# The first token tile alone up to its experts, the second beside the first expert slots, in a two-part transformer kernel

## Time and profile before

| what | value |
|---|---|
| median of 3 runs | 1614.35 us |
| profiled execution, whole | 1615.83 us |
| its span, first to last instruction | 1614.0 us |
| granted clock of TensorE, mean | 0.964 of full |
| busy: PE, DVE, ACT, POOL | 84%, 69%, 33%, 24% |
| moved by DMA | 433.17 MB, 268.45 MB of it by the gathers |

### The profile page before, as it was taken

One profiled execution on the slowest core, in us unless ns is written; L12 is line 12 of the kernel. 1 busy time (PEld: TensorE's weight loads), 2 busy tenths in 40 slices (PEclk: granted clock), 3 DMA queues, 4 the chain that ended last, 5 costly groups with the idle time before them and its releaser, 6 DMA issues.

```text
span 1614.0 us, 17165 instructions
## 1 busy us (share of the span) xinstructions
PE 1358.5 (84%) x6258; PEld 952.2 (59%) x6258; DVE 1108.2 (69%) x2039; ACT 532.0 (33%) x1030; POOL 384.5 (24%) x329
## 2 busy tenths in 40 slices
PE   5999788888876776777777779978999989899997
PEld 5887566444432222222232248857999878689996
DVE  6575588888656776888865565557756578767654
ACT  1443344332212112212221133543543254435430
POOL 1000003444433444444444401100111034001110
PEclk8899899999999999999999999989999999999999
DMA  9554528999999998999999954325545534255540
GB/s 365 211 209 157 209 79 323 381 411 399 421 413 382 418 422 340 422 420 422 421 411 422 422 222 157 105 79 185 209 168 198 185 131 139 97 196 196 195 170 26
DMA packets 116628, 433.17 MB, mean 268 GB/s; under 512 B 6832, under 2 KB 7088, under 8 KB 83520
## 3 DMA queue, kind: packets, MB, share of 16 engines
q0 software_dynamic: 36864, 268.45, 40.4%
q1 hardware_dynamic: 79392, 162.51, 28.3%
q10 hardware_dynamic: 288, 1.11, 0.2%
HBM read 431.00 MB, written 1.05 MB: 268 GB/s over the span
## 4 chain that ended last, share of the span: by engine, by line
PE 47%; DMA 25%; DVE 20%; ACT 5%; issue 2%; POOL 1%; SPq 0%; DVEq 0%; ACTq 0%; POOLq 0%
PE PS L1360 33%; DMA EB<-in_experts,EI 23%; DVE EB L2375 5%; DVE WL L2056 4%; PE PS L1560 4%; PE PS L1561 3%; PE PS L1345 2%; PE PS L1356 1%; PE PS L1343 1%; DVE LNV L2079 1%; DMA W<-in_w_ada 1%; DVE XL L2064 1%; ACT BIG L1878 1%; ACT WH L1702 1%; PE PS L1403 1%
## 5 line engine op out<-in xcount | busy, mean ns | idle before, releaser
L2652 POOL DMA_INDIRECT EB<-in_experts,EI x256 | 293.8, 1148 | 574.7 <-PE PS L1561 332.0
L1560 PE MATMUL PS<-EB,BIG 128*128 128x512 f32 x512 | 284.1, 637 | 161.1 <-ACT BIG L1878 160.8
L2375 DVE CUSTOM_DVE_ANT_0 EB<-EB,Y 128x1024 f32<-128x1024 f32 x256 | 313.5, 1225 | 139.1 <-DMA EB<-in_experts,EI 138.5
L2056 DVE TENSOR_TENSOR WL<-W,WH 128x1024 fp32r<-128x1024 f32 x232 | 299.3, 1338 | 100.7 <-ACT WH L1702 100.3
L1560 PEld LDWEIGHTS PS<-EB,BIG 128*128 128x128 f32 x512 | 89.5, 196 | 321.9 <-ACT BIG L1878 269.3
L1561 PE MATMUL PS<-EB,BIG 128*128 128x512 f32 x512 | 270.4, 611 | 0.0
L1702 ACT ACTIVATE WH<-W 128x1024 fp32r<-128x1024 f32 x232 | 229.5, 1048 | 80.1 <-PE PS L1356 73.3
L1360 PE MATMUL PS<-XH,WH 128*128 128x256 f32 x768 | 221.5, 288 | 6.1 <-DVE WL L2056 5.4
L1360 PE MATMUL PS<-XL,WH 128*128 128x256 f32 x768 | 216.7, 282 | 0.0
L1360 PE MATMUL PS<-XH,WL 128*128 128x256 f32 x792 | 215.2, 286 | 0.0
L1561 PEld LDWEIGHTS PS<-EB,BIG 128*128 128x128 f32 x512 | 100.4, 196 | 128.7 <-issue 128.7
(11 more groups left out here) (328 smaller groups left out, 1725.3 us busy)
## 6 DMA issues: line engine op xcount, KB each, us to landing
W<-in_ffn_w SPq DMA_DIRECT2D x32, 2048.0 KB, 8.7
W<-in_w_ada SPq DMA_DIRECT2D x12, 2048.0 KB, 13.1
W<-in_w_in SPq DMA_DIRECT2D x6, 2048.0 KB, 14.1
W<-in_hy_w_in SPq DMA_DIRECT2D x6, 2048.0 KB, 10.9
W<-in_gla_w_in SPq DMA_DIRECT2D x6, 2048.0 KB, 8.0
W<-in_w_query SPq DMA_DIRECT2D x4, 2048.0 KB, 10.5
W<-in_w_out SPq DMA_DIRECT2D x2, 2048.0 KB, 8.0
EB<-in_experts,EI POOLq DMA_INDIRECT x256, 10.9
```

The costliest lines, as they stand in the source:

```text
L1560: e.matmul(PS[u[0][0]][:, :], DG[i], rows_up[:, 1024:1536], start=start, stop=stop)
L2056: e.tensor_tensor(tile.lo[:, k, :], tile.w[:, k, :], tile.hi[:, k, :].bitcast(F32), ALU.subtract).then_inc(*VE.up(("lo", tile.index, n)))
L2375: e.tensor_tensor_reduce(out=u, in0=u, in1=Y[:, s // 128, :], scale=1.0, scalar=0.0, op0=ALU.mult, op1=ALU.add, accum_out=dots[:, s:s + 1] ...
L2652: e.indirect_dma_start(out=EBUF[i], out_offset=None, in_=A["experts"][:, :], in_offset=bass.IndirectOffsetOnAxis(ap=EI[:, t, j:j + 1], axi ...
```

## The change

- The fox heads are done per token tile: `forgetting(t, u)` does only the causal block of tile 0 (128 columns) or the 256 columns of tile 1. Tile 0's run stays in the hooks of win[5]. The tile's own norm, output products, x1 and transposes follow at once, and then its first two query tiles. Tile 1's sb half of the output product stands before tile 0's x1 is turned.
- Tile 1's fox heads, norm, output, x1 and all other query products and scores become one list of steps, `second_way`, of which the slot loop takes one at every even slot below 20, one at each of slots 20 to 42 and 50 to 56, and one at every even slot from 58 on; the list ends at slot 100.
- The output and query weights are no longer split: `wout_part` and `query_product` multiply float32 as it is, from one copy XT of the turned activations. A query product has the weights stationary, so its result is already turned, and the copy and four turns behind the first product go.
- Query tiles 1 and 2 are loaded as halves into the upper parts of two buffers by `load_query`; query tiles 0 and 3 share one buffer.
- The gathers use a ring of six buffers in slots 0 to 25; the two others, where the fox heads' data lies, join at slot 26 (JOIN).
- The late modulation tiles (`late_rows`) stand behind tile 1's first choice instead of ahead of it.
- Small moves: the keys are loaded earlier, the final gain at slot 112 instead of 76, clearing of query buffers is four writes instead of two.

```diff
+JOIN = 26
...
+        in_buf, had_buf, ring, last_slot = [], [], collections.deque(range(6)), {}
+        for s in range(SLOTS):
+            if s == JOIN:
+                ring.extendleft((7, 6))
+            b = ring.popleft()
+            ring.append(b)
...
-            norm_x1 = Norm("x1", do.x1_piece, x1_stats, do.x1_apply, Y)
-            later_split(wq[0])
...
+            square, first, second = fox_norm_steps(0, fox_u, lambda: at(4))
+            square()
             for j in range(2):
+                wout_group(j, 0, bank())
+            first()
+            second()
+            for j in range(2):
+                wout_rest(j, 0)
+                do.x1_piece(j, groups[j, 0], 0, ("tm", wout[j].index, 0))
+            for j in range(2):
+                wout_group(j, 1, at(6 + j))
+            x1_stats(0)
+            do.x1_apply(0)
+            x1_turned(0)
+            do.load_query(1)
...
+            def second_tile():
+                u = bank()
+                o.filling.add(u[0])
+                yield from forgetting(1, u)
+                square, first, second = fox_norm_steps(1, u, bank)
+                square()
+                o.filling.discard(u[0])
+                yield
+                first()
+                yield
+                second()
+                yield
+                for j in range(2):
+                    wout_rest(j, 1)
+                    yield
+                    do.x1_piece(j, groups[j, 1], 1, ("tm", wout[j].index, 1))
+                    yield
+                do.load_query(2)
+                x1_stats(1)
+                yield
+                do.x1_apply(1)
+                yield
+                x1_turned(1)
+                yield
+
+            def second_way():
+                yield from second_tile()
+                for t, j in ((0, 2), (1, 0), (0, 3), (1, 1), (1, 2), (1, 3)):
+                    yield from query(t, j, blocks=1)
...
-                for step in beside.pop(s, ()):
-                    step()
-                if s == 76:
+                if s < 20 and s % 2 == 0 or 20 <= s < 43 or 50 <= s < 57 or s > 57 and s % 2 == 0:
+                    next(way, None)
+                if s == 112:
                     do.fetch_gf()
...
-                    if t == 0:
-                        for j in (10, 11):
-                            yield from late_rows(j)
+                        if (t, h) == (1, 0):
+                            for j in (10, 11):
+                                yield from late_rows(j)
...
+            def wout_part(j, t, u, half):
...
+                for k in range(4 * half, 4 * half + 4):
+                    x, w = XT[:, k, block(t)], tile.w[:, k, :]
...
+                        e.matmul(PS[u[0]][:, :], x, w, start=k == 0, stop=False)
...
+            def query_product(t, j, i, u):
...
+                mm(PS[u[0]][:, block(i)], [(query_rows(j, k)[:, block(i)], XT[:, k, block(t)]) for k in range(8)], *names)
...
+            def fox_scores(h, t, u):
+                j = 2 * h + t
+                dve.wait_ge(TE, ("fox scores", t, h))
+                e.tensor_reduce(MXA[:, j:j + 1], PS[u[0]][:, 0:128 * (t + 1)], X_AXIS, ALU.max, negate=True).then_inc(
+                    *VE.up(("fox max", t, h)))
```

More of the change, by code:

```diff
@@ L695, in program, with put_v @@
             steps = collections.deque(head_norm_steps("sb", 1, values["sb"], gain=gain_sb, to=0)[:7])
+            passes = [0]
             def fox_pass():
-                if next(fox, True):
-                    return False
+                for _ in range((2, 1, 3, 2)[passes[0]]):
+                    next(fox, None)
+                passes[0] += 1
                 if len(steps) > 2:
                     steps.popleft()()
[L702 to L706, removed]
+            def put_v(u, t):
+                do.put_tokens(VF[t], win[5], t, u)
+                do.note(("v fox", t))
+            tm_tile(win[5], put_v, hook=fox_pass, n=3)
+            while steps:
+                steps.popleft()()
+            for _ in fox:
+                pass
+            while o.behind:
+                tick()
             groups = {}
@@ L710, in wout_group, with wout_rest, fox_norm_steps, square @@
                 groups[j, t] = u
[L711 to L721, removed]
-            assert not steps and len(groups) == 2
-            fox_steps = head_norm_steps("fox", 0, values["fox"], gain=gain_fox, to=1)
-            do.note("att")
-            tick(3)
-            for step in fox_steps[:4]:
-                step()
-            do.fetch_keys()
+                o.filling.add(u[0])
+                do.wout_part(j, t, u, 0)
+            def wout_rest(j, t):
+                u = groups[j, t]
+                do.wout_part(j, t, u, 1)
+                o.filling.discard(u[0])
+                if t:
+                    close_tile(wout[j])
+            def fox_norm_steps(t, u, to_bank):
+                k = slice(8 * t, 8 * t + 8)
+                hs, hr, ht = (a[:, 0:16] for a in (hs_, hr_, ht_))
+                def square():
+                    do.heads_write("fox", t, u)
+                    do.heads_square("fox", 0, t, u)
+                def first():
+                    do.heads_sums("fox", 0, t, u, 8, hs)
+                    do.rsqrt_first(("fox", t), hr[:, k], hs[:, k], 8 / 512, 1e-6, None)
+                def second():
+                    do.rsqrt_second(("fox", t), hr[:, k], hs[:, k], ht[:, k])
+                    do.heads_scale("fox", 0, t, 8, hr)
+                    turn_whole(to_bank(), Y[:, t, :], t, 0, ("ready", "fox", t), ("xt", "fox", t), gain_fox, 1)
+                return [square, first, second]
             def x1_stats(t):
@@ L892, in program @@
+            def second_way():
+                yield from second_tile()
+                for t, j in ((0, 2), (1, 0), (0, 3), (1, 1), (1, 2), (1, 3)):
+                    yield from query(t, j, blocks=1)
+            way = second_way()
+            next(way)
+            choice = choices()
             for _ in range(21):
                 next(choice)()
-            beside = collections.defaultdict(list)
-            for n, step in zip((1, 2, 3, 3, 4), (copy[1], keys[0], put[0], keys[1], put[1])):
-                beside[n].append(step)
@@ L962, in program @@
                     split_piece(hyt[0])
-            assert nu == SLOTS and chosen and not beside
+            assert nu == SLOTS and chosen and next(way, None) is None
             o.held = None
```

484 lines of the change are left out of this document (230 added, 254 removed).

## The result

The changed kernel takes 1633.28 us (median of 4 runs, 1629.37 to 1636.13), the one before 1614.34 beside it. The ratio is 1.0116, with a 95% interval of 1.0094 to 1.0137: slower, where -7 us was forecast. The profiled execution took 1633.01 us with a span of 1631.2, so the span grew by 17.2 us.

What follows compares the result with a forecast made beforehand. The prediction took the expert stage as bound by the gathers, 2.49 us a slot. Its terms, -28 + 9.5 + 11.5 + 7 - 7 = -7, gave 1606.5 us; the 8-in-10 range was 1589 to 1625.

Steps and rivals of the forecast that it cites:

- Term 1: Stage ahead of the slots: first gather at 224 us instead of 252.15, -28 us (bounds 218 and 232).
- Term 2: Slots 0 to 20, one tile 1 fox step per slot pair: rounds of 8 us, +9.5 us (bounds -6 and +20).
- two ups are 3.42 us: In each round of slots 0 to 20, PE's two up products take 3.42 us, ending at 6.8 us.
- the first dot comes 7 us after the first gather: At slot 0: 7 us, not 10.5, since no query tile is being loaded then.
- E + 3.4: In a round, E is the end of a head's scores on PE; ACT's diagonal, needed by the odd slot's up, ends 3.4 us later.
- rival B: Slots 0 to 57: hand-overs between DVE, PE and ACT take more than the front won; slower, 1628 us, 22% chance.
- Term 3: Slots 20 to 29, tile 1's norm, output and x1 read serially: 34 us against 22.3, +11.5 us (bounds 0 and +20).
- waits about 6 us: DVE in slots 20 to 29: waits for the turn 1, two output products 1.5 each, squares and root 2 us.
- the root with its table: In slots 20 to 29, DVE's wait for squares and the root including its table load: 2 us.
- term 4: Slots 29 to 57, query steps one a slot make PE exceed the gathers: +7 us together (bounds 0 and +13).
- term 5: Slot 128: POOL's wait for tile 1's first choice goes, -7 us with the refill behind it.
- The rule on the drain: Table switches on ACT: a 1.38 us drain beside the 1.28 load, 1.4 us more a round, 1616 us; 3 in 100.

Runs made afterwards that it cites:

- e2: The changed kernel with each tile 1 head's values product repeated six more times on PE while it waits for the diagonal; 1628.97 us, ratio 1.0079.
- e4: The changed kernel with tile 1's fox maxima, exponentials and copies one step behind their scores, in eleven steps instead of ten; 1618.31 us, ratio 1.0014.
- e5: The changed kernel with all ten fox steps of tile 1 between the choice steps ahead of slot 0; 1620.12 us, ratio 1.0032 to the kernel before.
- e7: e5 with tile 1's norm, output and x1 steps at every third slot from 1, and the last two buffers joining at slot 10; 1608.11 us, ratio 0.9958.
- e10: e7 with the seventh and eighth buffer joining at slot 26, as in the changed kernel, instead of 10; 1614.42 us, ratio 0.9994.
- e6: The changed kernel with copies in place of logarithm and exponential in tile 1's fox norm and x1 roots (wrong values); 1632.39 us, ratio 1.0107.
- e12: The changed kernel with only the query steps moved, one at every odd slot from slot 29 on; 1641.80 us, ratio 1.0166 to the kernel before.
- e1: The kernel before with one edit: late modulation rows stand behind tile 1's first choice of experts; 1609.30 us, ratio 0.9968.
- e3: The changed kernel with Square in place of Gelu in the slots, so no table change in the rounds; 1615.55 us, ratio 1.0001.

## Why the prediction was wrong

**Term 1 was right**, in its sub-steps too: x1's sum at 200.20 (200), the first maximum at 211.97 (212), the gather at 223.74 (224). The earlier sub-steps were within 2 us: PE ends the product that closes tile 9 at 182.5 (180.5) and the two sb halves at 189.4 (189).

**Term 2 failed, mis-sized by 16.6 us, in the steps "two ups are 3.42 us" and "the first dot comes 7 us after the first gather".** The first one: the prediction followed the round at full clock, though the same text has PE held until E + 3.4 for a diagonal, and its own rows showed a product twice as long behind idle time. It had used that for term 1 and for rival B only. The five regular pairs take 45.9 us from dot 4 to dot 14, not 40: 5.9 us, of which 4.9 go when PE is kept busy (e2).

The second one is 4.5 us: dot 0 is at +11.5. I had put the wait before down to a load of a query tile, but DVE works on the 21 steps of choice right up to its first dot, before and after, and no row of the trace has it wait for a transfer there. In the changed kernel one fox step stands ahead of these choices, and DVE, in its order, takes the maximum of head 0 first. Its scores stand on PE behind the second query tile:

```profile
226.51 0.42 DVE L2255 TENSOR_REDUCE ST<-PS 128x1 f32<-128x256 f32 x1 [3.70 <-PE PS L1549]
```

This wait of 3.70 us, and one of 0.73 behind it for the gates' exponential on ACT, are as long as the miss. No run takes them away: in e4 this maximum stands later, but DVE then waits 3.23 us for the exponential, and dot 0 comes 1.6 us sooner.

The other 6.2 us are 4.0 in slots 14 to 20, at 3.2 us and not 2.5, and 2.2 that are left for the first two pairs. No run parts the causes of slots 14 to 20: they take 17.0 to 19.6 us in e2 to e5 as well. DVE waits there twice for rows (1.58 and 1.16 us) and once for a gelu (1.98), and e7, with two more buffers, takes 17.6 us where e10 takes 21.0. The forecast's own sum is loose here, too: from +54, six slots at 2.5 end at +69, not +72.5. By its own steps term 2 would have been +6.

**Term 3 failed, the step "waits about 6 us"**: the waits were 11.8 us, and the term was mis-sized by 6.1. DVE's own work was right: 39.9 us less its waits of 11.8 leave 28.1, and 27.4 had been counted. The waits on DVE in this stretch (time, times, longest):

```profile
DVE XT L2120 <- PE PS L1432: 4.3, 1, 4.3
DVE Y L2304 <- PE PS L1446: 3.2, 2, 2.6
DVE XT L2118 <- PE PS L1432: 2.2, 1, 2.2
DVE BIG L2439 <- ACT BIG L1916: 1.3, 1, 1.3
DVE EB L2432 <- DMA EB<-in_experts,EI: 0.5, 1, 0.5
DVE ST L2090 <- ACT ST L1737: 0.3, 1, 0.3
```

Nothing waits long for the root itself. DVE waits for turns (4.3 and 2.2 us, 1 forecast) that stand on PE behind ups, which wait for diagonals that stand on ACT behind table loads:

```profile
313.42 1.28 ACT L1735 ACT_TABLE_LOAD   x1
...
315.91 1.28 ACT L1737 ACT_TABLE_LOAD   x1
...
317.49 1.28 ACT L1916 ACT_TABLE_LOAD   x1
...
319.06 1.28 ACT L1898 ACT_TABLE_LOAD   x1
...
321.23 1.28 ACT L1916 ACT_TABLE_LOAD   x1
```

Five loads in 9 us, where "the root with its table" counted one, and three more from 340.73 on for the root of x1. e6 leaves out six of these eight and wins 2.9 us, so that about half of the 6.1 stays without a shown cause. What share of it is PE's clock was not measured apart; PE waits 0.84 to 3.36 us for a diagonal five times in this stretch, and its granted clock is 0.83 from 300 to 320 us and 0.91 from 320 to 340. With the fox steps ahead, distance and two more buffers recover 5.6 and 8.3 us by slot 29 (e10, e7). The price of six buffers was no part of the sum beyond the 2.5 us a slot of term 2.

**Terms 4 and 5 were right** in size (6.8 for 7, 7.2 for 7) and in the main in cause, by e12's slots 29 to 57 and by e1. Slots 29 to 43 cost 1.9 us (1) and slots 43 to 57 4.9 (6). Of term 5, only 4.0 us come between the dots of 124 and 128, where POOL's wait was; 3.2 come between slots 64 and 124, and e1 has the same two parts (4.1 and 5.7). In between the distance to the kernel before is no measure: it runs through +4.1 us at slot 99, since three weight tiles are loaded from slot 68 on before and from slot 94 on now.

**The rule on the drain** (the Trainium skill, ScalarE: Activation LUTs, What ACT_TABLE_LOAD costs) would make a round longer by 1.4 us. The trace does not agree: gelu starts at 265.63, 0.02 us after the load ends (264.33 + 1.28), and the copy in front ended 0.07 us before it (263.88 + 0.38). The long rounds are longer by nearly the same amount, but on PE.

Rival B was the nearest and named the mechanism, but its numbers fit in part by luck. It had rounds of 9.5 us (9.2 in the mean), x1's slots at 4.5 us (4.4), and PE at clock 0.83 in the query slots, for 5 us more; there the granted clock was 0.96 (352.7 to 432.6 us), and term 4 stayed as forecast. The first dot and slots 14 to 20 took what that part didn't. The range, which ended at 1625, left out B's own 1628. Its chance of 22 in 100 was too low because I read the serial chain and the clock apart, though the wait of the one comes just ahead of the slow pairs of the other.

## What to carry to other kernels

Where a step is moved into a loop bound by transfers, write down the round trip over the engines; if PE idles in every round, give a range with PE's own work at the slow clock, too (here 8.2 or 9.85 us behind the same 2.64 us of idle time). Look at the first step of the list as well: what it hands to another engine may stand ahead of the work that starts the loop. Such a step is paid back by order: put the consumer one step behind the producer (e4), put the whole chain where another engine is busy anyway (e5), or give the ring more buffers (e7). Before filling slots that look free, ask which load and which deadline they cover (e12).

## What the runs showed of the hardware

- PE idles 2.64 us in each round of the changed kernel. In four of six rounds pairs of 512-column instructions behind it took up to 1.92 us, in the other two all took 1.02 to 1.12; the granted clock was 0.84 from 240 to 280 us. Where the wait was 1.57 us (e3) or 0.74 (e4), and where it was filled with work (e2), no pair behind it took more than 1.13. The levels are 1.2 and 2.4 GHz.
- Logarithm and exponential behind each other cost two table loads (313.42 and 315.91), and gelu after them a third (317.49).
- A table load took 1.28 us, and the function behind it started 0.02 us after its end (264.33 and 265.63).
